# Attention on both heads of a chunk at once in two stacked transformer blocks on one Trainium2 core, and a round that multiplies the last pair's values before it transposes the current one

## The reference, cut to what matters

```python
def block(q):                       # global, 128 queries at a time
    p = jax.nn.softmax(gqa_scores(q, k_all), axis=-1)
    return gqa_out(p, v_all)
# neighbourhood: softmax over [neighbours with bias, context]
# window: p = softmax([where(valid, scores, -1e30), context scores, sink])
# context queries (layer 0 only): softmax over the 256 context keys
def diff_attend(q, k, v, lam):      # block 2
    p = jax.nn.softmax(s, axis=-1)
    a = (p[:, :, 0] - lam * p[:, :, 1]).astype(v.dtype)
    return jnp.einsum('bhqk,bhkd->bhqd', a, v)
```

## Time and profile before

| | us |
|---|---|
| median of three runs | 2913.3 |
| lowest, highest | 2910.53, 2918.81 |
| the profiled execution's own time | 2914.16 |
| its span | 2912.4 |
| PE busy | 2730.9 (94%) |
| DVE busy | 1590.2 (55%) |
| ACT busy | 1156.9 (40%) |
| POOL busy | 150.7 (5%) |

### The profile page before, as it was taken

One profiled execution on the slowest core, in us unless ns is written; L12 is line 12 of the kernel. 1 busy time (PEld: TensorE's weight loads), 2 busy tenths in 40 slices (PEclk: granted clock), 3 DMA queues, 4 the chain that ended last, 5 costly groups with the idle time before them and its releaser, 6 DMA issues.

```text
span 2912.4 us, 39976 instructions
## 1 busy us (share of the span) xinstructions
PE 2730.9 (94%) x15308; PEld 2144.3 (74%) x15308; DVE 1590.2 (55%) x2657; ACT 1156.9 (40%) x2008; POOL 150.7 (5%) x164
## 2 busy tenths in 40 slices
PE   6999999999989899889999899999999799998897
PEld 3844578888765799668887447688886688776897
DVE  2454556563357687437762885533323686574554
ACT  2333344442344565432233622432222534543543
POOL 3000010000100000013000000100000210000000
PEclk9998999999999999989999999999999899998999
DMA  7244513323334355533222322132234433446555
GB/s 248 92 143 162 173 58 101 96 97 90 93 103 160 117 187 167 181 125 100 86 89 71 118 66 90 44 102 100 92 93 148 151 116 116 156 131 203 173 174 144
DMA packets 108746, 360.88 MB, mean 124 GB/s; under 512 B 12544, under 2 KB 14592, under 8 KB 108480
## 3 DMA queue, kind: packets, MB, share of 16 engines
q1 hardware_dynamic: 106592, 351.86, 37.5%
q0 software_dynamic: 2016, 7.12, 0.8%
HBM read 357.88 MB, written 1.05 MB: 123 GB/s over the span
## 4 chain that ended last, share of the span: by engine, by line
PE 86%; DVE 6%; ACT 3%; DMA 3%; issue 1%; POOL 0%; SPq 0%; POOLq 0%; DVEq 0%; ACTq 0%
PE bank L538 23%; PE bank L540 22%; PE bank L539 22%; PE bank L658 4%; PE bank L675 4%; PE bank L542 3%; PE bank L585 3%; PE bank L666 2%; PE bank L609 2%; DMA ring<-in_w_mod 2%; DVE rstd L1380 1%; DVE w_low L1286 1%; DVE smax L1431 1%; ACT w_high L881 1%; PE bank L618 1%
## 5 line engine op out<-in xcount | busy, mean ns | idle before, releaser
L538 PE MATMUL bank<-h_high,w_high 128*128 128x512 f32 (+1 forms) x2720 | 952.3, 350 | 56.6 <-DVE w_low L1286 30.7
L1286 DVE TENSOR_TENSOR w_low<-ring,w_high 128x1024 fp32r<-128x1024 f32 (+1 forms) x500 | 581.0, 1164 | 661.0 <-ACT w_high L881 659.8
L540 PE MATMUL bank<-h_high,w_low 128*128 128x512 f32 (+1 forms) x2720 | 938.8, 345 | 0.0
L539 PE MATMUL bank<-h_low,w_high 128*128 128x512 f32 (+1 forms) x2720 | 938.6, 345 | 0.0
L538 PEld LDWEIGHTS bank<-h_high,w_high 128*128 128x128 f32 x2720 | 520.3, 191 | 130.2 <-issue 34.5
L881 ACT CAST w_high<-ring 128x1024 fp32r<-128x1024 f32 (+1 forms) x500 | 488.3, 979 | 294.9 <-DMA ring<-in_w_down 162.6
L540 PEld LDWEIGHTS bank<-h_high,w_low 128*128 128x128 f32 x2720 | 519.8, 191 | 61.4
L539 PEld LDWEIGHTS bank<-h_low,w_high 128*128 128x128 f32 x2720 | 520.5, 191 | 60.0 <-issue 0.7
L538 PE MATMUL bank<-f_high,w_high 128*128 128x256 f32 (+1 forms) x704 | 237.0, 337 | 2.5 <-DVE w_low L1286 2.5
L539 PE MATMUL bank<-f_low,w_high 128*128 128x256 f32 (+1 forms) x704 | 236.5, 336 | 0.0
L540 PE MATMUL bank<-f_high,w_low 128*128 128x256 f32 (+1 forms) x704 | 236.5, 336 | 0.0
(11 more groups left out here) (181 smaller groups left out, 2802.9 us busy)
## 6 DMA issues: line engine op xcount, KB each, us to landing
ring<-in_w_mod SPq DMA_DIRECT2D x192, 512.0 KB, 4.0
ring<-in_w_up SPq DMA_DIRECT2D x176, 512.0 KB, 3.6
ring<-in_w_down SPq DMA_DIRECT2D x64, 384.0 KB, 3.1
ring<-in_w_gate SPq DMA_DIRECT2D x48, 512.0 KB, 3.6
ring<-in_w_down SPq DMA_DIRECT2D x64, 320.0 KB, 2.9
ring<-in_w_mix SPq DMA_DIRECT2D x16, 512.0 KB, 4.2
ring<-in_w_glu SPq DMA_DIRECT2D x16, 512.0 KB, 4.5
ring<-in_w_q SPq DMA_DIRECT2D x16, 512.0 KB, 3.6
```

Of the source, the lines that this page charges most:

```text
L538: pe.matmul(out, wh[:, cols], high, start=first, stop=False)
L539: pe.matmul(out, wh[:, cols], low, start=False, stop=False)
L540: ins = pe.matmul(out, wl[:, cols], high, start=False, stop=last)
L1286: v.tensor_tensor(wl[:, cols], raw[:, cols], wh[:, cols].bitcast(F32), ALU.subtract).then_inc(low_ready, 1)
```

## The change

In block 1 a unit becomes a pair: both heads of a chunk, for one query tile. `units_pair` gives two score matmuls, on the two halves of the partitions, two masks, two lists of value tiles and an output that covers all 128 partitions. Global, near and window then have 16 units each, and each round takes two slabs. Score banks are 2, 3, 4, 1 there, the output bank is 7 alone, and there are four buffers for turned probabilities instead of two. `turn(u)` makes two sets of transposes, `values(u)` alternates the two heads, tile by tile. In both blocks `values(u-1)` now stands ahead of `turn(u)`. The unit of block 2 is otherwise as it was. In the window stage a chunk is now complete every second round, and the last two chunks instead of one are split after the stage.

```diff
@@ tiles
+        PAIR_PROBT = PROBT + [SC[:, 2 + i, :] for i in range(2)]
+        PAIR_SCORES = [bank[i] for i in (2, 3, 4, 1)]
+        DIFF_SCORES = [bank[i] for i in (2, 3, 4, 0)]
-        OUTB = [bank[7], bank[1]]
+        OUTB = bank[7]
...
-        CHUNKS = {"global": (8, 0), "near": (8, 4), "window": (4, 0), "diff_0": (4, 0), "diff_1": (2, 0)}
+        CHUNKS = {"global": (4, 0), "near": (4, 4), "window": (2, 0), "diff_0": (4, 0), "diff_1": (2, 0)}
@@ PE
                 def scores(u):
+                    if u >= 2:
+                        pe.wait_ge(ex_ready, j0 + 2 * u - 2)
                     for i, (q, k) in enumerate(units[u]["subs"]):
-                        j = u * spu + i
-                        if j >= score_banks:
-                            pe.wait_ge(ex_ready, j0 + j - score_banks + 1)
-                        pe.matmul(SCORES[j % score_banks][:, 0:units[u]["T"]], q, k, start=True, stop=True).then_inc(sc_done, 1)
+                        pe.matmul(banks[(2 * u + i) % 4][:, 0:units[u]["T"]], q, k, start=True, stop=True).then_inc(sc_done, 1)
 
                 def turn(u):
...
+                    for i in range(sets):
+                        k = sets * u + i
+                        pe.wait_ge(pr_ready, t0 + k + 1)
+                        if k >= 2:
+                            pe.wait_ge(pt_ready, t0 + k - 1)
+                        src = PROB[(2 * u + 2 - sets + i) % 6]
+                        for t in range(units[u]["T"] // P):
+                            ins = pe.transpose(bank[5 + k % 2][:, t * P:(t + 1) * P], src[:, t * P:(t + 1) * P], IDENT)
+                        ins.then_inc(tr_done, 1)
 
                 def values(u):
-                    pe.wait_ge(pt_ready, u0 + u + 1)
-                    if u0 + u >= 2:
-                        pe.wait_ge(o_ready, u0 + u + 1 - len(outs))
+                    pe.wait_ge(pt_ready, t0 + sets * (u + 1))
+                    if u0 + u:
+                        pe.wait_ge(o_ready, u0 + u)
...
+                    for t in range(last + 1):
+                        for i, rows in enumerate(unit["rows"]):
+                            ins = pe.matmul(OUTB[rows, 0:P], unit["v"][i][t],
+                                            probt[(sets * u + i) % len(probt)][:, t * P:(t + 1) * P],
+                                            start=(t == 0), stop=(t == last))
...
-                    turn(u)
                     if u:
                         values(u - 1)
+                    turn(u)
@@ ACT
                 def copy(u):
...
+                    for i in range(sets):
+                        k = sets * u + i
+                        act.wait_ge(tr_done, t0 + k + 1)
+                        if u >= 2:
+                            act.wait_ge(pv_done, u0 + u - 1)
+                        nc.scalar.copy(probt[k % len(probt)][:, 0:w], bank[5 + k % 2][:, 0:w]).then_inc(pt_ready, 1)
@@ ACT, after the stage (DVE the same with low_out)
-                high_out(KC - 1)
+                for c in range(7 - l, KC):
+                    high_out(c)
@@ DVE
                 def normalise(u):
...
                     if not unit["diff"]:
                         v.tensor_scalar(p0, p0, r0, None, ALU.mult).then_inc(pr_ready, 1)
+                        v.tensor_scalar(p1, p1, r1, None, ALU.mult).then_inc(pr_ready, 1)
                         return
...
                 def store(u):
                     dve.wait_ge(pv_done, u0 + u + 1)
-                    v.tensor_copy(units[u]["out"], outs[u % len(outs)][units[u]["rows"], 0:P]).then_inc(o_ready, 1)
+                    v.tensor_copy(units[u]["out"], OUTB[:, 0:P]).then_inc(o_ready, 1)
```

More of the change, by code:

```diff
@@ L428, in units_diff @@
                             for i in range(2)]
-                    out.append(dict(subs=subs, T=keys.stop - keys.start, mask=None, diff=True, sink=None,
-                                    v=[VT[:, k0 + t, h * P:(h + 1) * P] for t in range((keys.stop - keys.start) // P)],
-                                    rows=slice(0, P), out=O[:, h, qt * P:(qt + 1) * P]))
+                    out.append(dict(subs=subs, T=keys.stop - keys.start, masks=None, diff=True, sink=None,
+                                    v=[[VT[:, k0 + t, h * P:(h + 1) * P] for t in range((keys.stop - keys.start) // P)]],
+                                    rows=[slice(0, P)], out=O[:, h, qt * P:(qt + 1) * P]))
             return out
@@ L646, in attend @@
                 units, beside = ATT[name], BESIDE[name]
-                outs = OUTB[0:1] if units[0]["diff"] else OUTB
-                pace = len(units) // (16 * len(beside))
-                spu = len(units[0]["subs"])
-                j0, u0 = n["sub"], n["unit"]
-                score_banks = 2 + spu
+                diff = units[0]["diff"]
+                sets = 1 if diff else 2
+                banks, probt = (DIFF_SCORES, PROBT) if diff else (PAIR_SCORES, PAIR_PROBT)
+                slabs = 16 * len(beside)
@@ L669, in values @@
                 def values(u):
-                    pe.wait_ge(pt_ready, u0 + u + 1)
-                    if u0 + u >= 2:
-                        pe.wait_ge(o_ready, u0 + u + 1 - len(outs))
+                    pe.wait_ge(pt_ready, t0 + sets * (u + 1))
+                    if u0 + u:
+                        pe.wait_ge(o_ready, u0 + u)
                     unit = units[u]
-                    for t, v in enumerate(unit["v"]):
-                        ins = pe.matmul(outs[u % len(outs)][unit["rows"], 0:P], v,
-                                        PROBT[u % 2][:, t * P:(t + 1) * P], start=(t == 0), stop=(t == len(unit["v"]) - 1))
+                    last = unit["T"] // P - 1
@@ L683, in attend @@
                         scores(u + AHEAD)
-                    if u % pace == 0:
-                        k = u // pace
+                    for k in range(u * slabs // len(units), (u + 1) * slabs // len(units)):
                         if k == 16:
@@ L698, in attend @@
                         stored()
-                n["sub"] += len(units) * spu
+                n["sub"] += len(units) * 2
                 n["unit"] += len(units)
+                n["turned"] += len(units) * sets
             def chunk_ready(count=KC):
@@ L1062, in attend @@
                 for u in range(len(units)):
-                    if u == 16 * pace and len(beside) == 2:
+                    if u == half and len(beside) == 2:
                         mod_copy(beside[0])
@@ L1423, in maxima @@
                     w = unit["T"]
-                    for i in range(spu):
-                        j = u * spu + i
+                    for i in range(2):
+                        j = 2 * u + i
                         dve.wait_ge(sc_done, j0 + j + 1)
-                        sc = SCORES[j % score_banks]
-                        if unit["mask"] is not None:
-                            own.link(v.tensor_tensor(sc[:, 0:S], sc[:, 0:S], unit["mask"], ALU.add))
+                        sc = banks[j % 4]
+                        if unit["masks"] is not None:
+                            own.link(v.tensor_tensor(sc[:, 0:S], sc[:, 0:S], unit["masks"][i], ALU.add))
                         m = smax[:, j % NS:j % NS + 1]
@@ L1541, in _ @@
                     attend("window", finish=low_out, opens="mix1_1")
-                low_out(KC - 1)
+                for c in range(7 - l, KC):
+                    low_out(c)
                 residual(f"mix1_{l}", w)
```

80 lines of the change are left out of this document (34 added, 46 removed).

## The result

The changed kernel took 2818.47 us (median of four runs, 2816.42 to 2820.53) beside 2911.91 us for the kernel before (2910.29 to 2918.81): a ratio of 0.9675 [0.9657, 0.9693], 93.4 us less. The forecast was 2829, 10.5 us more. The profiled execution took 2819.43 us, its span 2817.6 us, at a mean granted clock of 0.966.

A forecast was written before the change was run, and what follows sets the result against it. PE was taken to bound block 1's three stages, with DVE taking over in window. Global -30.5, near -30.5, window -27.5 and first differential stage +3 make -85.5; 2914.2 - 85.5 = 2829 us, range 2806 to 2860.

The forecast's parts named there:

- Pairs of scores cost what one did: Block 1: the second head's score matmuls are free, saving 1.05 us a long pair and 0.63 a short one.
- Pairs of values cost what one did: Block 1: two heads' value matmuls run side by side, 1.02 us a long pair and 0.58 a short one.
- PE's rounds of 4.07 and 2.78, a chunk 13.7: Block 1, PE us per long and short pair (6.40 and 4.26 before), and per chunk in global and near.
- Near: Near stage: 65.9 us where 96.4 stood, -30.5, PE still bounding and the 11.1 us loss of before kept.
- the paired work ends the low stretch at once: Block 1 stages: paired work ends the low granted clock at once; up to 20 us come back, 2809 us.
- Window: Window stage: DVE becomes the bound at 4.51 us a round; 79.3 us for 106.8, -27.5.
- diff_0: First differential stage: new order makes values wait for the store behind normalise; +3 us, bounds -7.5 to +10.
- diff_1: Last differential stage: PE-bound with the same operations, so 0 us change.
- Its store is 0.7 us ahead of need: Last differential stage: the store comes 0.7 us before it is needed, supporting the forecast of 0.
- Loads: Rival, global and near: slab loads become the bound, +4 to +12 us, 2833 to 2841; chance 0.10.
- low clock: Rival, three block 1 stages: granted clock stays at half speed, 2977 us; chance 0.04.
- values in turn: Rival, block 1: two heads' values don't run side by side, 2857 us; chance 0.08.

The follow-up runs named there:

- e4: Changed kernel with the two modulation slabs of a round put between the first and second head's score matmuls in block 1; 2866.17 us, ratio 0.9834.
- e11: Changed kernel with a round's transposes put between the first and second head's value matmuls in block 1; 2854.02 us, ratio 0.9798.
- e9: Changed kernel with block 1's modulation slab matmuls cut from 256 to 64 columns, loads kept; 2813.59 us in one execution.
- e8: Changed kernel without the window stage's mask additions on DVE; 2816.99 us in one execution.
- e2: Kernel before with only the order changed, values of the previous unit ahead of the transposes, in both blocks; 2920.48 us, ratio 1.0026.
- e1: Changed kernel with the old order, transposes ahead of the previous pair's values, in both blocks; 2814.90 us, ratio 0.9665.
- e7: Changed kernel with DVE's store of the previous unit ahead of the next unit's normalisation, in all stages; 2813.53 us, ratio 0.9650.
- e5: Kernel before with only the first differential stage's modulation slabs moved from even to odd rounds; 2913.51 us, ratio 1.0001.
- e10: Changed kernel with DVE's store ahead of the normalisation in both differential stages and the old order in the last; 2820.21 us, ratio 0.9681.
- e12: Changed kernel with DVE's store ahead of the normalisation in the first differential stage only, and the old order in the last; 2815.91 us, ratio 0.9669.
- e3: Changed kernel with a pair's value matmuls issued head by head instead of alternating; 2828.41 us, ratio 0.9701.

## Why the prediction was right, point by point

- **Pairs of scores cost what one did**: held. 1.06 for four records, and without it (e4) 47.7 us of the gain are lost. The row of the differential stage was the right one to read it from.
- **Pairs of values cost what one did**: held, and was the real bet, since no row showed it. 1.02 and 0.59 against 1.02 and 0.58 forecast; e11 prices it at 33 us in block 1. The slabs on four column strips had been the right neighbour. The Trainium skill's rule that a change of the tiling mode drains the engine (TensorEngine Tiling (Array Packing), Key Properties) fits, 0.58 against 0.49 for transposes; in e11, which adds a change of shape to each round, nothing more of it shows, since every piece took 1.02.
- **PE's rounds of 4.07 and 2.78, a chunk 13.7**: measured 4.09 in the window stage and a chunk of 14.1 in global (0.28 of it a wait). Forecast 59.9 for global, measured 59.1 (a saving of 31.2 for 30.5).
- **Near**: forecast 65.9, measured 62.7 (a saving of 33.5 for 30.5). I left the loss of before (11.1 us) in place. The stretch at the lower clock shrank from 23.9 to 10.2 us, whose half, 6.9, is more than the difference of 3.0; that the longer lead-in of pairs takes the rest back is argued, not shown. The alternative that I had named ("the paired work ends the low stretch at once") did not happen either: 10.2 us stayed low, and the stage lies nearer to the forecast than to the 54.8 of that case.
- **Window**: the term that was mis-sized, 79.3 against 73.7. That DVE becomes the bound was right (e9), but its round is 4.18 on average, not 4.51, and 16 x 0.33 = 5.3 of the 5.6 us are that. Two scalings that don't depend on each other take 0.80 together, where my sum has 2 x 0.48 (and the earlier trace rows shows 0.45, not 0.48); the store takes 0.20 and not 0.30; a `low_out` costs 0.34 each second round and not 0.42; the rest is rounding. My sum for the stage's end was also 0.2 too high as written (1.01 + 0.6 + 1.1 + 0.3 - 0.8 is 2.2, not 2.4). So DVE bounds by only 0.09 us a round, and with its masks gone the stage runs into PE at once (e8).
- **diff_0**: forecast +3, measured -0.5, and right only by half. The store's wait is there and costs +2.2 to +2.8 (e2, e1, e7). The slabs' new rounds give -2.8 (e5). That the slabs of this stage move was in the change, and no step of mine priced it. With the new rounds DVE waits for scores 4.2 us (e5, 7 times) where it waited 6.6, and PE for `normalise` 7.0 where it waited 9.8: some slabs now fill time in which PE waited for DVE, and no longer hold up scores that DVE waits for.
- **diff_1**: forecast 0, measured +1.2 (e2 and after alike). "Its store is 0.7 us ahead of need" held, but two things were overlooked. PE's round is 3.13 us with the new order and 3.09 with the old (before, e1), 0.4 over the stage: transposes take 0.53 ahead of scores and took 0.49 ahead of values. And from the last scores to the end of the stage it is 9.8 us for 9.0. The last values now follow their own transposes with nothing between, and wait for the copy out of PSUM, where before the last thing waited for was the store (0.48 us, L1458). In after:

```profile
2479.79 1.16 PE L679 MATMUL bank<-h_space,v_tokens 128*128 128x128 f32 x8 [0.68 <-ACT h_space L1066]
```

  The other stages of after have such a wait of 0.5 to 0.7 us at their end too (221.0, 285.8, 871.9, 1593.0 us).
- **Loads, low clock, values in turn**: the loads cost PE 0.7 us of idle time in two stages (3.4 us of waits of its weight loads), not 4 to 12; the clock rose rather than fell (0.97, 0.92, 0.98 for 0.94, 0.88, 0.97); the values run side by side. One reading behind the clock rival was off: PE's idles in the first differential stage of before were 0.57 and 0.83 us in two of four rounds, not 0.6 to 1.3 in each. The rule on small idles stands in the Trainium skill (TensorE: Matmul & The Clock Gate) under "A second HAM failure mode: psum-queue depth-cycling", not in the section that I named. In before and after this stage kept 1.00; in e10, e11 and e12 it had 6.8 us at 0.50 from 4.6 us after its first scores on, which cost some 2.7 us. What set that off is open.

Sum: forecast -85.5, measured in the span -94.8. Of the 9.3 between them the window round is 5.3, near 3.0, diff_0 3.5 and global 0.7, less 1.2 for diff_1 and 2.3 outside the stages; the small rest is at the window's ends. So the total came closer than its parts, which is luck: some 13 us of error one way met 3.5 the other way.

Open: why the stretch at the lower clock at a stage's start has the length that it has. It goes with single-head scores and moved a stage by over 2 us between kernels with the same instructions there (near of after and e12, 10.2 and 3.4 us low, 62.73 and 60.33 us). Not tried: a second output bank in the differential stages, since no bank is free there.

## What to carry to other kernels

When a matmul fills half of the array's rows or columns, look for the other half of the work and issue the two as neighbours, alternating piece by piece: here scores were worth 48 us and values 33, of 2912. Then the round must be summed again on every engine, since the second one (DVE, whose round in the window stage is now 0.09 us longer than PE's) and the loads (0.7 us of idle PE) stand close by. A change in the order of one engine is priced by who waits for the moved piece at the steady round, at the stage's end, and against the order of the engine that it meets; an order that saves nothing where PE is full cost 0.26% by itself (e2).

## What the runs showed of the hardware

- Two 64-column matmul chains into the two column halves of one bank, float32: 1.02 us when they alternate, 1.51 head by head as neighbours, 2.04 apart. The second head's first record starts before the first head's last three, so PE takes up matmuls out of their order, though not far (shown by the starts of single records in e3 alone; which head a record belongs to is read from its place in the two rows).
- Two 64-row matmuls with 512 columns into two banks: 1.06 us together (after), 1.05 each, 2.10 in all, with slabs between (e4).
- DVE scalings of 128 by 512 float32 show 0.49 us each and start 0.40 apart; a record's length is not its price.
- In near PE was granted half speed (0.50) for 23.9 us in before, with single-head scores and no idle time of PE in that stretch (the earlier trace rows shows 20 us of it), 16.7 in e2, and for 3.2 to 10.2 us with pairs; in e4, where only the scores were put apart again, for 17.1.
